# A new order of the steps in the second block of a two-block transformer kernel: mixer and attention steps of both layers, and the third output panel by input pairs

## The reference

```python
for l in range(2):
    if l == 1:
        kv = rmsnorm(h, kv_norm) @ w_kv
        k = rmsnorm(heads(kv[..., :256]), k_norm); v = heads(kv[..., 256:])
    proj = rmsnorm(h, norm_mix[l]) @ w_in[l]
    main, mq = proj[..., :768], proj[..., 768:]
    if l == 0:
        main_out = pool_mixer(main, pool_w[0], pool_scale[0])       # window means, 4 groups
    else:
        q = rmsnorm(heads(main), q_norm)
        main_out = swa_sink_attention(q, k, v, sinks)                # 12 query heads, window 128
    mkv = rmsnorm(mem, mem_norm[l]) @ w_mem_kv[l]                    # 4 memory heads
    mem_out = softmax(rmsnorm(heads(mq)) @ rmsnorm(heads(mk)).T / 8) @ mv
    h = h + concat([main_out, mem_out]) @ w_out[l]
    h = h + relu(rmsnorm(h, norm_mlp[l]) @ w_up[l]) ** 2 @ w_down[l]
```

## Time and profile before

| what | value |
|---|---|
| median of 3 runs | 1132.51 us (1126.26 to 1134.53) |
| the profiled execution | 1128.03 us |
| span in its profile | 1126.2 us |
| TensorE matmuls busy | 1047.2 us (93%) |
| VectorE busy | 686.4 us (61%) |
| ScalarE busy | 549.7 us (49%) |
| GpSimd busy | 88.9 us (8%) |
| mixer part of the second block, first layer | about 531 to 639 us |
| mixer and attention part, second layer | about 821 to 947 us |

### The profile page before, as it was taken

One profiled execution on the slowest core, in us unless ns is written; L12 is line 12 of the kernel. 1 busy time (PEld: TensorE's weight loads), 2 busy tenths in 40 slices (PEclk: granted clock), 3 DMA queues, 4 the chain that ended last, 5 costly groups with the idle time before them and its releaser, 6 DMA issues.

```text
span 1126.2 us, 20502 instructions
## 1 busy us (share of the span) xinstructions
PE 1047.2 (93%) x8556; PEld 1004.3 (89%) x8561; DVE 686.4 (61%) x807; ACT 549.7 (49%) x714; POOL 88.9 (8%) x64
## 2 busy tenths in 40 slices
PE   4998999899898999999879799999999888999998
PEld 3987789899797899999878799999998778999998
DVE  5677355644667777777843765555576656555554
ACT  4546345253544565556633544343475455544442
POOL 0050021100020000000271100000020001000000
PEclk9999899999999999999889899999999999999999
DMA  6534233234261554555232355555544222555551
GB/s 241 202 136 150 76 112 113 76 113 150 87 234 61 174 216 177 195 192 199 97 113 87 103 193 179 192 180 191 183 150 145 81 75 93 208 187 186 204 177 67
DMA packets 24803, 168.77 MB, mean 150 GB/s; under 512 B 2753, under 2 KB 3137, under 8 KB 5154
## 3 DMA queue, kind: packets, MB, share of 16 engines
q1 hardware_dynamic: 23616, 164.64, 41.9%
q10 hardware_dynamic: 1122, 3.19, 0.9%
HBM read 166.76 MB, written 1.05 MB: 149 GB/s over the span
## 4 chain that ended last, share of the span: by engine, by line
PE 72%; DVE 15%; ACT 9%; issue 3%; DMA 1%; SPq 0%; ACTq 0%; DVEq 0%
PE G L570 12%; PE G L572 11%; PE G L571 11%; PE D L570 7%; PE D L572 7%; PE D L571 7%; DVE wlo L1687 5%; ACT whi L1187 3%; PE M L570 2%; PE M L572 2%; PE M L571 2%; PE D L808 1%; DVE cv L2051 1%; PE M L794 1%; PE M L812 1%
## 5 line engine op out<-in xcount | busy, mean ns | idle before, releaser
L1687 DVE TENSOR_TENSOR wlo<-raw,whi 128x2048 fp32r<-128x2048 f32 (+1 forms) x156 | 360.5, 2314 | 162.1 <-ACT whi L1187 162.0
L570 PE MATMUL G<-xh,whi 128*128 128x256 f32 (+1 forms) x1360 | 391.2, 288 | 24.6 <-DVE xl L1708 9.6
L571 PE MATMUL G<-xl,whi 128*128 128x256 f32 (+1 forms) x1360 | 382.4, 281 | 0.0
L572 PE MATMUL G<-xh,wlo 128*128 128x256 f32 (+1 forms) x1360 | 382.2, 281 | 0.0
L1187 ACT ACTIVATE whi<-raw 128x2048 fp32r<-128x2048 f32 (+1 forms) x156 | 295.5, 1897 | 58.2 <-PE D L572 54.5
L570 PEld LDWEIGHTS G<-xh,whi 128*128 128x128 f32 (+1 forms) x1360 | 258.8, 190 | 35.0 <-issue 15.2
L571 PEld LDWEIGHTS G<-xl,whi 128*128 128x128 f32 (+1 forms) x1360 | 259.0, 190 | 1.6 <-issue 1.5
L572 PEld LDWEIGHTS G<-xh,wlo 128*128 128x128 f32 (+1 forms) x1360 | 258.4, 190 | 0.0
L570 PE MATMUL D<-hh,whi 128*128 128x256 f32 x688 | 191.4, 278 | 2.8 <-DVE wlo L1687 1.7
L571 PE MATMUL D<-hl,whi 128*128 128x256 f32 x688 | 191.2, 278 | 0.0
L572 PE MATMUL D<-hh,wlo 128*128 128x256 f32 x688 | 191.2, 278 | 0.0
(11 more groups left out here) (373 smaller groups left out, 1347.1 us busy)
## 6 DMA issues: line engine op xcount, KB each, us to landing
raw<-wall_dram SPq DMA_DIRECT2D x152, 1024.0 KB, 4.9
raw<-wnarrow_dram SPq DMA_DIRECT2D x4, 768.0 KB, 4.2
x<-x_dram SPq DMA_DIRECT2D x4, 256.0 KB, 5.5
mem<-mem_dram ACTq DMA_DIRECT2D x1, 1024.0 KB, 5.3
out_dram<-x SPq DMA_DIRECT2D x4, 256.0 KB, 2.5
poolw<-pool_w_dram ACTq DMA_DIRECT2D x1, 576.0 KB, 7.1
cst<-cst_dram ACTq DMA_DIRECT2D x1, 416.0 KB, 9.2
lora<-lora_dram ACTq DMA_DIRECT2D x1, 256.0 KB, 6.8
```

The lines of the kernel that those rows point to most:

```text
L570: mm(out, w_h, hi, start=start, stop=False, skip_group_check=skip)
L571: mm(out, w_h, lo, start=False, stop=False, skip_group_check=skip)
L572: return mm(out, w_l, hi, start=False, stop=stop, skip_group_check=skip)
L1687: signal(tt(wlo[:, pan.slot, 0:w], raw[:, pan.slot, 0:w], f32(whi[:, pan.slot, 0:w]), SUB), "w_lo")
```

## The change

The table `W` is written anew from the first panel of the second block on, and some functions with it. The computation is the same.

- `begin` is now a step of TensorE alone; the split ahead of time is a step of its own, `ahead p`, on ScalarE and VectorE. All eight `wout` panels now have a `begin` and an `ahead` (before, the first two of `wout1` had a `begin`); `in0m+2` has lost its `begin` and `in0m+3` has one.
- ScalarE's exponentials of the memory heads are a step of their own, `exp_m`, apart from `score_m`. In the second layer the squares of the keys (`hn_square 2`) now stand ahead of them.
- The outputs of `pv_m` and `pv_s` are read in steps of their own (`out_m`, `out_s`).
- `mem_norm` is cut into `mem_scale` (the eight L2098 instructions) and the split. `mem_scale 1` stands behind panel `in0q`, the split of layer two's memory behind `out_m 0`; both stood ahead of the third `wout0` panel.
- `soft_m 0` stands ahead of the split at `in0m+2`, `soft_m 1` behind `hn 2`, a split and the reading of the values. `hn 1` stands behind panel `in1` instead of ahead of it.
- In the final norm of the first block VectorE makes `xl` of one pair while it scales the next ones.
- The third `wout` panel is ordered by input pairs: its first half needs the third pair only, its second half the fourth. The weights are laid out to match on the host.
- The queries' sums use bank M0 instead of M1; the transposed heads use G0, G1, M1, G0 in group 0 and D0 to D3 in groups 1 and 2 (before: G0, G1 in turn, and D0, D1 in turn); the attention's products use D2, D3, D0 (before: D2, D3, D2).

```diff
+    TURNED = (("G0", "G1", "M1", "G0"), ("D0", "D1", "D2", "D3"))
+    SUMMED = ("D2", "D3", "D0")
...
-          ("soft_m", 1), ("begin", k1 + 1), ("hn", 2), ("panel", k1 + 1), ("begin", q2), ("turn_p", 1),
+          ("hn_square", 2), ("begin", k1 + 1), ("exp_m", 1), ("hn", 2), ("ahead", k1 + 1), ("panel", k1 + 1), ("soft_m", 1),
+          ("begin", q2), ("ahead", q2), ("turn_p", 1), ("panel", q2), ("square_s", 1), ("turn_v",), ("score_s", 0),
...
             for half in halves:
-                at = 2 * (i - 2) + half
-                for n in range(2):
-                    for kq in range(4):
-                        k = 2 * order[2 + kq // 2] + kq % 2
...
+                if i < 3:
+                    pe.wait_ge(S("xl"), XLN[name] - 3 + i + (half if i == 2 else 0))
+                if i == 0:
+                    free(banks[2 * half])
+                    free(banks[2 * half + 1])
+                for at in (2 * half, 2 * half + 1) if i < 2 else (0, 1) if i == 2 else (2 + half,):
+                    pairs_in = (i,) if i < 2 else (2 + half,) if i == 2 else (2, 3)
...
-        def begin(p):
-            if WHAT[p][0] in AHEAD:
-                split_to(p + 3)
+        def ahead(p):
+            split_to(p + 3)
...
         def final_norm():
             for i in range(4):
                 scaled(x, x, rstd, "fin_g", i, "x_ready", 0)
+                if i:
+                    part(3, i - 1)
+            part(3, 3)
...
         def panel(p):
             name, i = WHAT[p]
+            if name == "in0m":
+                read(p)
             if name not in OUTS:
                 split_to(p + 3)
...
-        def mem_norm(l):
+        def mem_scale(l):
...
-        late = t[:, :, 2:].reshape(2, PT, P, P)
-        return np.concatenate([panels(t[:, :, i].reshape(-1, P, P)) for i in range(2)] + [panels(late.reshape(-1, P, P))])
+        return np.concatenate([panels(u.reshape(-1, P, P)) for u in
+                               (t[:, :, 0], t[:, :, 1], t[:2, :, 2:].transpose(2, 0, 1, 3, 4, 5), t[2:, :, 2:])])
```

129 lines of the change are left out of this document (62 added, 67 removed).

## The result

The changed kernel took 1125.99 us (median of 20 runs, 1114.2 to 1131.3) beside 1129.4 us of the kernel before on the same chip (20 runs, 1124.8 to 1137.5). The ratio is 0.994, 95% interval 0.9914 to 0.9966: a gain of 3.8 to 9.7 us, where I had forecast 15. The profiled execution took 1128.88 us, its span is 1126.6 us: no shorter than the 1126.2 of the profile before.

A forecast was written before the change was run, and what follows sets the result against it. Chains crossing VectorE and ScalarE leave TensorE idle or at low clock in the mixer parts, some 46 us. Gains of 12 (layer one) and 3 (layer two) make 15: 1113 from 1128.0, 1117.5 from 1132.5; forecast 1115, range 1102 to 1127.

The forecast's parts named there:

- The diagonals: Layer one, memory heads: split moved behind the diagonals removes most of TensorE's 5.82 us wait, 4, plus 2 of clock: 6.
- The third panel by pairs: Layer one's third output panel: first half needs only the third pair; wait of 2.0 goes, 1 for clock: 3 gained.
- The exit wait: Wait of 5.1 us for x ahead of layer one's feed-forward: 1.8 left, 3.3 gained.
- The start of the layer: Layer one: scalings ahead of the keys' norm delay TensorE 4 us, a half panel fills 2.8; 1 lost, 0 to 3.
- the eight scalings: Memory scaling on VectorE, layer one's start: 3.25 us, nothing added as GpSimd's sums are over; otherwise one more GpSimd instruction.
- The three new waits: Layer two, TensorE: new waits of 6.1 us for dgm, 2.2 for D2, 2.7 for group 1's diagonals.
- The waits that were to go: Layer two: dg wait falls from 4.7 to 3.0; waits of 3.1 (third diagonals), 1.6 (xl), 1.5 (third output panel) go.
- small gaps: Layer two's attention: about 2 us more gained where a copy or a bank was waited for, none over 1 us.
- rival A: New layer-two waits each bring 2 us of low clock; layer two ends 5 behind, 7 gained, 1123 us; chance 0.17.
- D: Rival: splits hide behind loads, layer one gains only its 5.1 and 2.0 us waits, 1126 us; chance 0.09.
- Rival C: Low clock stays in layer two from the memory heads' diagonals to group 1; slower, 1139 us; chance 0.06.
- my own signs of being wrong: Layer one's wait for the keys' norm over 5 us, layer two over 126 us, or gaps ending with a panel's load.

The follow-up runs named there:

- x5: Changed kernel with VectorE's split ahead of layer one's memory-head diagonals again; layer one's mixing part 100.8 us, one execution 1132.8 us.
- x7: Changed kernel with the third output panel's first half waiting for both last input pairs; mixing parts 98.8 and 127.8 us, one execution 1130.2 us.
- x9: Changed kernel with layer two's memory scaled where VectorE stood idle ahead of the first pool panel; layer one's mixing part 90.2 us, one execution 1120.5 us.
- x6: Changed kernel with layer two's memory scaled and split late again, ahead of the third output panel's split; layer one's mixing part 95.7 us, one execution 1123.6 us.
- x4: Changed kernel with the queries' sums back on bank M1; mixing parts 98.2 and 123.5 us, ratio to the kernel before 0.9934.

## Why the prediction was half right

The order of steps did what most of the working said; the sum was too high by 6.5 us, 4.2 of it in layer two and 2.3 in layer one.

**Layer one, forecast 12, measured 9.7.** The diagonals: forecast 6, x5 says 4.3. The times were close: I had `dgm` ready at 585.1, which is 586.9 on the new profile's clock, where the layer starts 1.8 us later, and it came at 587.7; TensorE did a half panel more and had no wait. The third panel by pairs: forecast 3, x7 says 2.3. The exit wait: forecast 1.8 left, measured 2.85, since the third pair's low parts took 1.88 beside other work where I had 0.9. The start of the layer: this is the badly sized step. "Of these 4 us a half panel fills 2.8. I take this start as 1 us lost." TensorE waited 3.61 us for `ht` in spite of the half panel, because the scaling began at 559.27 and took 3.73. The next small matmuls and the panel behind them ran at the lower clock (8.2 us instead of 5.7). x9 gave 6.3 us by taking the scaling away from there. It did not sink layer one's sum only because the same cost stood there before in another form (2.6 waited for `ht` at L612), and because the early memory pays 6.4 at the exit (x6). x5, x7 and x6 account for 5.8 of the 9.7; the remaining 4 should lie in the early half panels and the place of the squares and sums, which I did not take apart.

On the eight scalings I had written that GpSimd's sums would be over. They were not: its last sum ended at 559.94, 0.7 us into the scaling, which took 3.73 where x9's, alone, took 3.25. So it cost half a us and not one more instruction of GpSimd, as I had written; that sum took 2.13 us, and only its last 0.7 were left. By the Trainium skill, "SBUF — State Buffer", on the engine side, the two engines' port pair is an exclusive lock, and the later one waits for the other's whole instruction; the half us is of the size of that overlap, and no run here shows the lock by itself.

**Layer two, forecast 3 gained, measured 1.2 lost.** The three new waits came as worked out: `dgm` 6.0 (forecast 6.1), D2 2.3 (2.2), group 1's diagonals 3.3 (2.7). The waits that were to go (4.7, 3.1, 1.6 and 1.5) went. The 4.7 even went to nothing where I had 3.0, but only because TensorE was held up just before: without that hold (x4) 2.6 of it stand there, near my 3.0. The step that failed is the phrase "and about 2 more in small gaps, none over 1 us". There was a gap of 3.0 us. The memory values' product writes M0. The change had moved the sums of squares to M0, and VectorE reads the second group's sums out of it behind the first group's scores, their maximum and a split, at 881.83:

```profile
879.62 2.28 DVE L1687 TENSOR_TENSOR wlo<-raw,whi 128x2048 fp32r<-128x2048 f32 x1
881.83 0.16 DVE L2121 TENSOR_TENSOR qa<-M,qe 128x8 f32<-128x8 f32 x1
```

The product starts 0.05 us after that addition. x4 moved the bank and got 3.3 us back, net of those 2.6. I had treated the new bank as a name without a queue: of the one edit in the change that touches no order, I priced only what it frees. The rest is clock. I counted 2.3 behind the wait for `dgm` (6.49 instead of 3.73 is 2.8), and nothing behind the 3.0 and the 3.3, where the rows show 0.8 and 0.8 for the product and the half panel behind it (2.78 and 3.83 us, against 2.00 and 3.01 in x4) and 2.5 for the turned heads (5.46 us against 2.94 for the next group; 4.54 in x4 behind the same wait). A further 1.0 us is the wait for x at the end, 2.6 where it was 1.6, which stands nowhere in my sum.

**The time itself.** Forecast 1115, measured 1126, inside the range of 1102 to 1127. In its total rival A comes nearest: 7 gained, where the profiles show 8.5, and given back in layer two, in part by the low clock behind the new waits that it names and in part by a wait that it lacks. Its division is not what happened: it had 12 in layer one and 5 lost in layer two, measured 9.7 and 1.2, and the later waits did shrink. D's number, 1126, was met by chance, since by its mechanism layer one would have gained the waits of 5.1 and 2.0 only, and the diagonals alone gave 4.3 (x5). Rival C (the low clock stays) did not happen. Of my own signs of being wrong one came, layer two longer than 126 us, and the wait for x stayed above the 2.5 that I had named (2.85).

Of the 15 us, 8.5 are there in the profiles, 3.4 and 9.5 in the two pairs of medians. The third step that failed is a term put at nothing: the pace of the feed-forward parts. My showed one stretch, and I took it for all of them ("223 matmuls in 25 us, so 0.112 us each"). The middle part of the same profile held 215, and the fast distance itself is 0.113. The pace is why the profile after is no shorter than the one before: its last part took 186.7 us against 179.2, 7.5 more. The unchanged first block did the rest, which ended 1.8 us later (533.2 against 531.4). That the distance between 3.4 and 9.5 is pace too is likely and not shown, since only one execution of each run was profiled.

## What to carry to other kernels

When an edit moves a result to another bank or buffer, write down who reads it out and behind what that reader stands, and then who wants to write there next: a bank is a queue like an engine. A step that is moved away from a wait should go where its engine is idle for at least its length (4.49 us were there for a scaling of 3.25), not merely earlier. And before a change of one per cent is judged, take the profile twice and compare the stages, cut at the same instruction, since two profiles of one kernel differed here by as much as the change.
